# One weight array in order of use, loaded in 4 KB rows, in a four-half-layer transformer trunk

## The reference, cut to what matters

```python
def swiglu(x, w_gate, w_up, w_down):
    return (jax.nn.silu(x @ w_gate) * (x @ w_up)) @ w_down

for i in range(DEPTH):                                   # DEPTH = 2
    h = swiglu(x, ffn_w_gate[i, 0], ffn_w_up[i, 0], ffn_w_down[i, 0])
    x = layer_norm(ALPHA * x + 0.5 * h, ln_g[i, 0], ln_b[i, 0])
    y = chunked_rel_attention(...) if i == 0 else stick_breaking_attention(...)   # w_qkv, w_o
    x = layer_norm(ALPHA * x + y, ln_g[i, 1], ln_b[i, 1])
    h = swiglu(x, ffn_w_gate[i, 1], ffn_w_up[i, 1], ffn_w_down[i, 1])
    x = layer_norm(ALPHA * x + 0.5 * h, ln_g[i, 2], ln_b[i, 2])
```

## Time and profile before

| | us |
|---|---|
| median of 3 runs | 982.34 (981.73 to 982.75) |
| the profiled execution, device time | 982.12 |
| its span, first to last instruction | 980.4 |
| PE busy | 967.9 (99% of the span) |
| DVE busy | 643.2 (66%) |
| ACT busy | 487.4 (50%) |
| DMA, mean over the span | 187 GB/s |
| SP's queue (q1), packets | 146320 packets, 173.56 MB, 54.5% of 16 engines |

### The profile page before, as it was taken

The page is one execution under the profiler, slowest core; times in us unless marked ns, Lnnn a source line. Parts: engine busy times, 40 slices in busy tenths (PEclk is TensorE's granted clock), DMA queues, the critical chain, the costliest instruction groups (busy, mean ns, idle before and its releaser), DMA issues.

```text
span 980.4 us, 13660 instructions
## 1 busy us (share of the span) xinstructions
PE 967.9 (99%) x5190; PEld 812.8 (83%) x5190; DVE 643.2 (66%) x760; ACT 487.4 (50%) x603; POOL 41.9 (4%) x72
## 2 busy tenths in 40 slices
PE   8999999999999999999999999999999999999996
PEld 6888888887877888888888888888878788888885
DVE  5666774676667766664676666638777676667635
ACT  5555562356663555563345555433656445555530
POOL 1100000010101000000000000001111100000000
PEclk9999999999999999999999999999999999999999
DMA  9956556576452665557555655754854546565611
GB/s 316 304 172 197 188 200 230 172 212 202 158 172 84 218 198 187 192 194 255 174 172 175 200 182 194 261 166 134 239 167 142 159 139 205 172 198 187 239 62 43
DMA packets 149243, 182.84 MB, mean 187 GB/s; under 512 B 5936, under 2 KB 128976, under 8 KB 149200
## 3 DMA queue, kind: packets, MB, share of 16 engines
q1 hardware_dynamic: 146320, 173.56, 54.5%
q0 software_dynamic: 2592, 8.17, 2.6%
q10 hardware_dynamic: 288, 0.52, 0.2%
HBM read 181.16 MB, written 1.07 MB: 186 GB/s over the span
## 4 chain that ended last, share of the span: by engine, by line
PE 93%; DVE 2%; issue 2%; ACT 2%; DMA 1%; POOL 0%; POOLq 0%; SPq 0%; DVEq 0%; ACTq 0%
PE psum L432 30%; PE psum L436 15%; PE psum L378 12%; PE psum L380 12%; PE psum L379 12%; PE psum L541 5%; PE psum L544 2%; PE psum L581 1%; PE psum L366 1%; PE psum L591 1%; ACT w_hi L678 1%; PE psum L603 1%; DMA raw<-in_ffn_w_up 1%; ACT probs L785 0%; DVE w_lo L874 0%
## 5 line engine op out<-in xcount | busy, mean ns | idle before, releaser
L874 DVE TENSOR_TENSOR w_lo<-raw,w_hi 128x2048 fp32r<-128x2048 f32 x162 | 369.2, 2291 | 193.7 <-ACT w_hi L678 193.4
L432 PE MATMUL psum<-xT,w_hi 128*128 128x512 f32 x1280 | 402.3, 396 | 0.0
L678 ACT ACTIVATE w_hi<-raw 128x2048 fp32r<-128x2048 f32 x162 | 307.3, 1907 | 98.7 <-PE psum L380 98.6
L436 PEld LDWEIGHTS psum<-xT,w_lo 128*128 128x128 f32 x1280 | 240.5, 188 | 56.8
L436 PE MATMUL psum<-xT,w_lo 128*128 128x256 f32 x1280 | 251.5, 278 | 0.0
L432 PEld LDWEIGHTS psum<-xT,w_hi 128*128 128x128 f32 x1280 | 195.2, 189 | 0.3
L378 PE MATMUL psum<-w_hi,hT_hi 128*128 128x512 f32 x416 | 163.3, 393 | 0.0
L379 PE MATMUL psum<-w_lo,hT_hi 128*128 128x512 f32 x416 | 162.0, 389 | 0.0
L380 PE MATMUL psum<-w_hi,hT_lo 128*128 128x512 f32 x416 | 162.0, 389 | 0.0
L722 ACT ACTIVATE hT_hi<-hiddenT 128x256 f32 (+1 forms) x80 | 33.4, 418 | 198.1 <-DVE hiddenT L903 198.1
L380 PEld LDWEIGHTS psum<-w_hi,hT_lo 128*128 128x128 f32 x416 | 78.1, 188 | 16.4
(11 more groups left out here) (79 smaller groups left out, 639.2 us busy)
## 6 DMA issues: line engine op xcount, KB each, us to landing
raw<-in_ffn_w_down SPq DMA_DIRECT2D x88, 512.0 KB, 4.1
raw<-in_ffn_w_gate SPq DMA_DIRECT2D x86, 512.0 KB, 4.0
raw<-in_ffn_w_up SPq DMA_DIRECT2D x86, 512.0 KB, 5.0
raw<-in_w_qkv_a SPq DMA_DIRECT2D x24, 512.0 KB, 5.4
raw<-in_w_qkv_b SPq DMA_DIRECT2D x24, 512.0 KB, 5.3
raw<-in_w_o_a SPq DMA_DIRECT2D x8, 512.0 KB, 4.3
raw<-in_w_o_b SPq DMA_DIRECT2D x8, 512.0 KB, 4.1
gain<-in_ln_g POOLq DMA_DIRECT2D x6, 512.0 KB, 3.8
```

The source lines that it names most:

```text
L432: pe.matmul(TILE[j][:, which, :], as_gu(w_hi[s])[:, k, at:at + P], xT[:, kk, :, :], start=kk == 0, stop=False)
L436: last = pe.matmul(TILE[j][:, which, 0:SEQ], as_gu(w_lo[s])[:, k, at:at + P], xT[:, kk, 0, :], start=False, stop=kk == KD - 1)
L678: act.activation(w_hi[slot][:], raw[raw_slot][:], ACT.Copy).then_inc(hi_done, 1)
L874: dve.tensor_tensor(w_lo[slot][:], raw[raw_slot][:], w_hi[slot][:], ALU.subtract).then_inc(lo_done, 1)
```

## The change

On the host, before the launch, all weights are laid out anew in one array `units` of 164 tiles, in order of use, each 128 rows of 8 KB. Row p of tile n is exactly what partition p of `raw` has to hold for unit n. On the chip each unit is two transfers of 512 KB, and each moves 4 KB per partition, one half of the 8 KB row. Units 0 and 1 take one transfer for each half, where there were two of 256 KB. SP's list has no loop any longer; every transfer is written out. The tiles in `raw`, the semaphores and their meaning, and the work of PE, DVE, ACT and POOL stay as they were, in the same order.

```diff
             def load_first():
                 for n in range(2):
                     for load in range(2):
                         k = 2 * load
-                        for w, at in ((w_gate, 0), (w_up, CHUNK_F)):
-                            src = w[0, 0, (4 * n + k) * P:(4 * n + k + 2) * P, 0:CHUNK_F]
-                            sp.dma_start(as_gu(raw[n])[:, k:k + 2, at:at + CHUNK_F],
-                                         src.rearrange("(k p) n -> p k n", p=P)
-                                         ).then_inc((early_loaded[n], raw_loaded[n])[load], 16)
+                        sp.dma_start(as_gu(raw[n])[:, k:k + 2, :], as_gu(units[n])[:, k:k + 2, :]
+                                     ).then_inc((early_loaded[n], raw_loaded[n])[load], 32)
                     if n == 0:
                         sp.dma_start(x[:, 1, :], x_in[0, P:SEQ, :]).then_inc(x_loaded[2], 16)
...
-            def load_rows(w, k0, n):
+            def load_unit(n):
                 s = n % RAW
-                slot_free(n)
-                for kk in range(2):
-                    sp.dma_start(as_rows(raw[s])[:, kk, :],
-                                 w[(k0 + kk) * P:(k0 + kk + 1) * P, :]).then_inc(raw_loaded[s], 16)
...
+                if n >= RAW:
                     slot_free(n)
...
+                for half in range(2):
+                    sp.dma_start(as_rows(raw[s])[:, half, :], as_rows(units[n])[:, half, :]
+                                 ).then_inc(raw_loaded[s], 16)
+
+            load_first()
+            for n in range(2, UNITS):
+                load_unit(n)
...
+    def gate_up(f):
+        w = np.stack([ffn_w_gate[f // 2, f % 2], ffn_w_up[f // 2, f % 2]])
+        w = w.reshape(2, 2, KD // 2, P, CHUNKS, CHUNK_F)
+        return w.transpose(4, 1, 3, 2, 0, 5).reshape(2 * CHUNKS, P, 2048)
...
+    units = np.concatenate([part for m in range(DEPTH) for part in (ffn(2 * m), mixer(m), ffn(2 * m + 1))])
```

More of the change, by code:

```diff
@@ L114, with build @@
 DIAG = 128
-def build(nc, x_in, w_qkv, w_o, rel_bias, w_gate, w_up, w_down, ln_g, ln_b, table, out):
+def build(nc, x_in, units, rel_bias, ln_g, ln_b, table, out):
     with ExitStack() as ctx:
@@ L229, in as_gu @@
         def as_gu(t):
-            return t[:].rearrange("p (k n) -> p k n", k=KD // 2)
+            return t.rearrange("p (k n) -> p k n", k=KD // 2) if isinstance(t, bass.AP) else as_gu(t[:])
         def as_qkv(t):
@@ L235, in as_rows @@
         def as_rows(t):
-            return t[:].rearrange("p (k n) -> p k n", k=2)
+            return t.rearrange("p (k n) -> p k n", k=2) if isinstance(t, bass.AP) else as_rows(t[:])
         def steps(f, c, j):
@@ L266, in slot_free @@
                 sp.wait_ge(lo_done, n - RAW + 1)
[L268 to L274, removed]
-                    for w, at in ((w_gate, 0), (w_up, CHUNK_F)):
-                        src = w[f // 2, f % 2, kh * HALF:(kh + 1) * HALF, bass.ds(c * CHUNK_F, CHUNK_F)]
-                        sp.dma_start(dst[:, :, at:at + CHUNK_F],
-                                     src.rearrange("(k p) n -> p k n", p=P)).then_inc(raw_loaded[s], 16)
             def load_first():
@@ L290, in load_first @@
                     if n == 0:
                         sp.dma_start(x[:, 1, :], x_in[0, P:SEQ, :]).then_inc(x_loaded[2], 16)
-            def load_rows(w, k0, n):
+            def load_unit(n):
                 s = n % RAW
-                slot_free(n)
-                for kk in range(2):
-                    sp.dma_start(as_rows(raw[s])[:, kk, :],
-                                 w[(k0 + kk) * P:(k0 + kk + 1) * P, :]).then_inc(raw_loaded[s], 16)
[L301 to L323, removed]
-                    slot_free(n)
[L325 to L338, removed]
+                if n >= RAW:
+                    slot_free(n)
+                for half in range(2):
[4 more added lines that the diff above has]
+                load_unit(n)
             for r in range(ROWS):
@@ L1166, with rows, mixer, ffn @@
     from concourse.bass_utils import run_bass_kernel_spmd
+    def gate_up(f):
+        w = np.stack([ffn_w_gate[f // 2, f % 2], ffn_w_up[f // 2, f % 2]])
+        w = w.reshape(2, 2, KD // 2, P, CHUNKS, CHUNK_F)
+        return w.transpose(4, 1, 3, 2, 0, 5).reshape(2 * CHUNKS, P, 2048)
+    def rows(w):
+        return w.reshape(-1, 2, P, D).transpose(0, 2, 1, 3).reshape(-1, P, 2048)
+    def mixer(m):
+        w, w_o = ((w_qkv_a, w_o_a), (w_qkv_b, w_o_b))[m]
+        w = w[0].reshape(KD, P, 3, D)
+        groups = rows(w_o[0])
+        made = []
+        for unit in MIX_ORDER:
+            if unit[0] == "v":
+                cols = slice(unit[1] * HALF, (unit[1] + 1) * HALF)
+                made.append(w[4 * unit[2]:4 * unit[2] + 4, :, 2, cols].transpose(1, 0, 2).reshape(P, 2048))
+            elif unit[0] == "qk":
+                cols = slice(unit[1] * P, (unit[1] + 1) * P)
+                made.append(w[:, :, 0:2, cols].transpose(1, 0, 2, 3).reshape(P, 2048))
+            else:
+                made.append(groups[unit[1]])
+        return np.stack(made)
+    def ffn(f):
+        return np.concatenate([gate_up(f), rows(ffn_w_down[f // 2, f % 2])])
+    units = np.concatenate([part for m in range(DEPTH) for part in (ffn(2 * m), mixer(m), ffn(2 * m + 1))])
     nc = bacc.Bacc("TRN2", target_bir_lowering=False, num_devices=1)
-    given = dict(x=x, w_qkv_a=w_qkv_a, w_o_a=w_o_a, rel_bias=rel_bias, w_qkv_b=w_qkv_b, w_o_b=w_o_b,
-                 ffn_w_gate=ffn_w_gate, ffn_w_up=ffn_w_up, ffn_w_down=ffn_w_down, ln_g=ln_g, ln_b=ln_b)
+    given = dict(x=x, units=units, rel_bias=rel_bias, ln_g=ln_g, ln_b=ln_b)
     arrays = {"in_" + name: np.ascontiguousarray(a) for name, a in given.items()}
@@ L1174 @@
     out = nc.dram_tensor("out", (1, SEQ, D), F32, kind="ExternalOutput").ap()
-    build(nc, t["x"], (t["w_qkv_a"][0], t["w_qkv_b"][0]), (t["w_o_a"][0], t["w_o_b"][0]), t["rel_bias"],
-          t["ffn_w_gate"], t["ffn_w_up"], t["ffn_w_down"], t["ln_g"], t["ln_b"], table, out)
+    build(nc, t["x"], t["units"], t["rel_bias"], t["ln_g"], t["ln_b"], table, out)
     return run_bass_kernel_spmd(nc, [arrays], core_ids=[0]).results[0]["out"]
```

## The result

The changed kernel takes 985.96 us (median of 7 runs, 985.05 to 986.6) against 982.34 before, also the median of 7. The ratio is 1.0035, with a 95% interval of 1.0026 to 1.0044: 3.6 us slower. Forecast were 981.6 us and a range of 980.6 to 983.0, so the time lies outside the range, and on the other side of the kernel before. The profiled execution took 985.22 us, with a span of 983.5, 3.1 us more than before. Among the experiments, one execution of e8 took 1611.89 us at a granted clock of 0.56 and is left out of its ratio.

The account below looks back on a forecast made before the run. PE was taken to bound the kernel, busy 967.9 of 980.4 us, with later loads hidden. The start gives 0.75 us: 982.12 - 0.75 = 981.4, the median 0.2 higher, so 981.6 us; range 980.6 to 983.0.

Parts of the forecast that it names:

- the matmul of 10.23 us: End of the start's chain, after which it stays on PE; forecast 0.75 us earlier, with nothing lost again behind it.
- the possible gain: At the start, 1.05 us at most, since x's way through PE, ACT and DVE takes until 9.2 us.
- step (4): At the start, what is late next: x's second half lands at 6.1 to 6.3 us, leaving 0.75 of 1.05 us.
- correction for the start from rest: At the start: landings reckoned from full-queue rates come up to 0.75 us too early.
- rival (B): 8 KB rows read by halves are slow for memory; at 250 GB/s at the start, 984.8 us; 5%.
- Step (3): ACT and DVE at the start: ACT copies block 0 at 5.84 us instead of 6.69, DVE's splits 0.85 us earlier.
- Rival (A): At the start, x becomes late instead of weights; break-even 1.1 us later; 0.4 us gained to 1.1 lost; 19%.

Follow-up runs that it names:

- e8: The changed kernel with the halves of units 0 and 1 in 2 KB rows, two 256 KB transfers for each half; 982.27 us.
- e1: The changed kernel with the halves of units 0 and 1 loaded in 1 KB pieces again, two 256 KB transfers for each half; 982.73 us.
- e10: The changed kernel with units 0 and 1 in contiguous 256 KB quarters of 2 KB rows, all other units in contiguous halves; 981.01 us.
- e2: The changed kernel with each half of a tile contiguous in memory, same 4 KB rows and transfers; 984.67 us.
- e6: The changed kernel with more identity multiplications on PE while it waits for x (WARM_UP 12, 4, 1 instead of 6, 1, 1); 984.70 us.
- e5: The changed kernel with x's first rows moved from ACT's queue to the head of SP's list; 984.38 us.
- e9: e5 with each half of a tile contiguous in memory as well; 983.69 us.

## Why the prediction was wrong

**What held.** PE's work and pace are untouched by the changed traffic; the 162 later units give nothing (e1); SP's longer list costs nothing; nothing behind the start moves against the rest; what happens before the matmul of 10.23 us is carried whole to the end. The size of the possible gain was right as well: e10 reached 1.0 of the 1.05 us.

**What failed is step (4).** It named the right transfer and the right mechanism, x's second half beside 4 KB packets, but mis-sized it: landing at 6.1 to 6.3 us, measured 9.38. Its share of about a third was right (0.24 of 0.82 MB). Three terms were wrong. The rate: I gave both queues 414 GB/s, a rate of full queues in mid-kernel, and x a third of that, 138 GB/s. From rest both together made 273 GB/s in 3 to 6 us, and x had 0.24 MB in those 3 us, 80 GB/s. I had a correction for the start from rest (0.75 us), taken from weights in 1 KB pieces, and applied it to the weights but not to x. The head start: I let x have 0.08 MB by 2.3 us, from the earlier trace rows, as if that stretch of the kernel before stayed what it was. Measured were 0.02 MB by 3.0 us. The other 0.50 MB at the 94 GB/s that x had over 3 to 8 us (0.47 MB) take until 8.3, and with the 0.6 us behind the last packet that makes 8.9, an estimate from these rows that comes near the 9.38. No run shows why the head start went; e1, in 1 KB pieces of the new array, had 0.10 MB by 3 us, and e2, in 4 KB rows without gaps, 0.03. And the gaps: I put their whole effect into rival (B) as a case by itself, with 5%, instead of as a term of the landing of x; they cost 90 of 328 GB/s in 2 to 6 us.

Step (3) failed with it, by x's first half. It took over the 5.82 us at which ACT is done with the first piece of x. But that half landed at 6.8 us instead of 4.7, so ACT waited, and split block 0 at 7.82 us, not at 5.84; it never waited for a weight:

```profile
7.54 0.38 ACT L680 ACTIVATE xT<-psum 128x256 fp32r<-128x256 f32 x1 [4.31 <-PE psum L317]
```

**Rival (A)** had its break-even right. x landed 3.4 us later than before; 1.1 of that is covered as the rival said, which leaves 2.3 us. But I let x fall to a fifth of 414 GB/s (83) at the outside, and saw no more than 1.1 us lost. The rate of 80 GB/s in 3 to 6 us is nearly that fifth; that x came at 9.38 and not at 8.2 us is the head start. The missing piece, some 0.5 us of the 2.8, is PE: the matmuls ahead of block 2 took 0.43 us (four of them) and 0.38 instead of 0.23, 0.9 us more in sum. A part of that is covered by DVE, which had block 2 split near 12.4 us. No step had priced PE's speed. e6 gave back 1.3 us by filling the pause.

**Rival (B)** was true in its mechanism and far from its price: without gaps e2 is 1.3 us faster. The warning of the Trainium skill on row pitch (DMA: Bandwidth & Descriptors, section Latency and other measured facts) is given for pitches from 512 KiB up, and the rate falls to half only at 4 and 8 MiB there (103 GB/s, where 2 MiB had 164 and a padded pitch 214), so the prediction put it too broadly with "a pitch of megabytes"; here a pitch of 8 KB, half of it read by each transfer, took the rate of the first microseconds from 328 to 238 GB/s and the median landing from 4.1 to 4.7 us. The step from "the pieces are 4 KB as in `w_down`" to "they move like `w_down`" was the mistake: `w_down`'s rows lie without gaps.

**The chances.** 5% for (B) and 19% for (A), as separate cases, missed that both act on the same transfer at the same time. The range ended at 983.0, since (A) was cut at what one cause could do.

**What stays open**: why a single queue with 4 KB rows is slow at the very start (e5, e9); why x lost its head start; why PE was fast at 4.68 us in e10 and slow at least up to 7.6 us in the kernel before, with the same multiplications ahead; and why the time of x's landing varies (9.38 in the changed kernel, 10.06 in e6, whose loads are the same).

## What to carry to other kernels

Where loads are hidden behind slot waits, look only at the first transfers, and price each by the rate from rest, with every queue that shares the engines: a small transfer in small packets beside large ones is what comes late. Keep the packets of the large transfer no larger than those of the urgent one beside it, and lay each transfer, not each tile, contiguously in memory: together that turned a loss of 3.6 us into a gain of 1.3 (e10). A late operand can cost PE twice, by the wait and by matmuls that stay slow longer (0.43 us instead of 0.23) because PE had nothing to do.

## What the runs showed of the hardware that was not expected

- Halves of 8 KB rows, 4 KB each: 238 GB/s in 2 to 6 us against 328 with the same 4 KB rows without gaps, and a median landing of 4.7 against 4.1 us over 328 transfers.
- x's 0.52 MB on ACT's queue was complete at 5.97 us beside 1 KB pieces, at 9.38 beside 4 KB rows with gaps, and at 8.26 beside 4 KB rows without; in 4 KB rows of its own, beside the ones with gaps, it was complete at 6.62.
- A single queue in 4 KB rows moved 188 GB/s in 3 to 6 us (e5), and 221 without gaps (e9), where two queues in 2 KB rows without gaps moved 356 (e10).
- PE's matmuls took 0.43 us up to about 12.9 us in the changed kernel, with pauses of 2.3 and 1.1 us before, at a granted clock that the profile gives as 1.00; in the kernel before they took 0.23 us from 8.44 us on. In e5, where PE had been fast (the last two multiplications of the identity took 0.39 us, as in e10) and then stood 2.9 us, they took 0.43 us, and the row of the clock shows 0.50.
